# Sharing the weight sums of the wide products between GpSimd and VectorE

## The reference

```
proj = x @ w_in            # 1024 x 9240; among its parts: oa, zb, gate_a, gate_b
ha = mlstm(qa, ka, va, gates)                       # rms norm, then times sigmoid(oa)
hb = gated_delta(conv(qkv_b), beta, a)              # rms norm, then times silu(zb)
y  = sigmoid(gate_a) * (ha @ w_branch_a) + sigmoid(gate_b) * (hb @ w_branch_b)
x  = layernorm(alpha * x + y @ w_out)
x  = layernorm(alpha * x + (silu(gate) * up) @ w_ffn_down)   # gate, up = x @ w_ffn_up
```

## Time and profile before

| | us |
|---|---|
| median of 3 runs | 2968.23 (2964.52 to 2969.87) |
| the profiled execution | 2973.33 |
| its span | 2971.0 |
| TensorE busy | 2755.1 |
| VectorE busy | 1234.2 |
| ScalarE busy | 605.4 |
| GpSimd busy | 377.9 |

### The profile page before, as it was taken

One profiled execution on the slowest core, in us unless ns is written; L12 is line 12 of the kernel. 1 busy time (PEld: TensorE's weight loads), 2 busy tenths in 40 slices (PEclk: granted clock), 3 DMA queues, 4 the chain that ended last, 5 costly groups with the idle time before them and its releaser, 6 DMA issues.

```text
span 2971.0 us, 31547 instructions
## 1 busy us (share of the span) xinstructions
PE 2755.1 (93%) x12368; PEld 1548.1 (52%) x12368; DVE 1234.2 (42%) x2182; ACT 605.4 (20%) x1191; POOL 377.9 (13%) x359
## 2 busy tenths in 40 slices
PE   6998899999999998978787999999999999999998
PEld 3455564454434555534333586665445686664453
DVE  2546532222324554211111253553665444554675
ACT  1134311111111142111111113341110113430110
POOL 2100000000001000000000004654000006562000
PEclk8999889999999998988888899999999999999999
DMA  9324238999999345899999643134335433224342
GB/s 286 94 90 158 85 142 342 421 421 421 421 421 316 122 177 220 358 422 421 421 421 421 221 156 125 61 114 133 127 141 210 144 140 114 87 84 170 142 156 99
DMA packets 182658, 670.22 MB, mean 226 GB/s; under 512 B 8113, under 2 KB 18665, under 8 KB 133361
## 3 DMA queue, kind: packets, MB, share of 16 engines
q1 hardware_dynamic: 175696, 653.28, 56.8%
q0 software_dynamic: 6816, 14.94, 2.1%
HBM read 667.09 MB, written 2.90 MB: 226 GB/s over the span
## 4 chain that ended last, share of the span: by engine, by line
PE 70%; DMA 19%; DVE 6%; ACT 3%; issue 2%; POOL 0%; SPq 0%; DVEq 0%; ACTq 0%; POOLq 0%
DMA ring<-in_exp_w_up_dram 19%; PE bank L801 18%; PE bank L813 10%; PE bank L1507 9%; PE bank L1402 7%; PE bank L1567 4%; PE bank L1421 4%; PE bank L320 3%; PE bank L1022 3%; PE bank L1230 2%; PE bank L1074 1%; PE bank L961 1%; PE bank L843 1%; PE bank L983 1%; PE bank L769 1%
## 5 line engine op out<-in xcount | busy, mean ns | idle before, releaser
L813 PE MATMUL bank<-ring,arena 128*64 128x512 f32 (+1 forms) x2992 | 593.6, 637 | 94.4 <-DMA ring<-in_exp_w_up_dram 77.7
L813 PEld LDWEIGHTS bank<-ring,arena 128*64 128x64 f32 (+1 forms) x2992 | 174.2, 128 | 492.2 <-issue 408.6
L801 PE MATMUL bank<-ring,arena 128*128 128x512 f32 (+1 forms) x764 | 318.6, 577 | 1.6 <-ACT arena L457 1.5
L1507 PE MATMUL bank<-ring,arena 128*128 128x512 f32 (+1 forms) x672 | 267.1, 557 | 3.9 <-issue 3.3
L1402 PE MATMUL bank<-ring,arena 128*128 128x512 f32 x560 | 260.0, 597 | 1.3 <-ACT arena L2043 1.3
L801 PEld LDWEIGHTS bank<-ring,arena 128*128 128x128 f32 x764 | 144.7, 191 | 166.0 <-issue 163.9
L801 PE MATMUL bank<-arena,ring 128*128 128x256 f32 x1024 | 222.7, 379 | 0.0
L3164 POOL TENSOR_TENSOR ring<-ring 128x512 f32<-128x512 f32 x160 | 213.8, 1336 | 46.3 <-PE bank L1402 34.8
L801 PEld LDWEIGHTS bank<-arena,ring 128*128 128x128 f32 x1024 | 193.6, 189 | 28.9 <-issue 0.9
L1507 PEld LDWEIGHTS bank<-ring,arena 128*128 128x128 f32 x672 | 126.6, 190 | 137.7 <-issue 135.0
L2591 DVE COPY arena<-bank 128x512 f32<-128x512 f32 x64 | 44.3, 692 | 369.0 <-PE bank L813 368.2
(11 more groups left out here) (351 smaller groups left out, 2979.0 us busy)
## 6 DMA issues: line engine op xcount, KB each, us to landing
ring<-in_exp_w_down_dram SPq DMA_DIRECT2D x64, 2048.0 KB, 19.2
ring<-in_exp_w_up_dram SPq DMA_DIRECT2D x63, 2048.0 KB, 23.7
ring<-in_exp_w_gate_dram SPq DMA_DIRECT2D x60, 2048.0 KB, 22.6
ring<-in_w_in_dram SPq DMA_DIRECT2D x42, 2048.0 KB, 7.8
ring<-in_ada_w_dram SPq DMA_DIRECT2D x24, 2048.0 KB, 11.6
ring<-in_w_ffn_up_dram SPq DMA_DIRECT2D x20, 2048.0 KB, 8.0
ring<-in_w_ffn_down_dram SPq DMA_DIRECT2D x10, 2048.0 KB, 8.0
ring<-in_w_out_dram SPq DMA_DIRECT2D x8, 2048.0 KB, 10.1
```

Of the source, the lines that this page charges most:

```text
L801: last = mm(o, lhs(k), rhs(k), start=start and k == 0, stop=stop and k == kt - 1)
L813: last = mm(U(us[c])[g * rows:(g + 1) * rows, :], lhs(k), rhs(i, c), start=(k < parts), stop=(k >= KT - parts))
L1507: last = mm(U(u)[:, 0:n], lhs(k), rhs[:, k, 0:n], start=(k == 0), stop=(k == 3))
```

## The change

The two sums of the upper blocks stay on GpSimd. The two sums of the lower blocks leave GpSimd's program and become one VectorE instruction of 128x2048 each. They stand in VectorE's second fill step of p7, which had no work before. There VectorE waits for p3, for the two counts of `pool_sums` and for the arrival of both slots. They count on a new semaphore, `low_sums`, on which TensorE waits before p6 and p4; before p5 and p7 it waits on `pool_sums` as it did. GpSimd no longer waits for p3 before its additions, other than for its being copied out.

```diff
@@ TensorE, dense()
-                            if name in ("p5", "p7", "p6", "p4"):
+                            if name in ("p5", "p7"):
                                 nc.tensor.wait_ge(sem["pool_sums"], pe.due("pool_sums"))
+                            if name in ("p6", "p4"):
+                                nc.tensor.wait_ge(sem["low_sums"], pe.due("low_sums"))
@@ VectorE, dense()
                         first = FIRST_PART[i % 2]
+                        top0 = slot[arrived[l, (i, 0)][0]][:, 0:4, :]
+                        low0, low1 = (slot[arrived[l, (i, c)][0]][:, 4:8, :] for c in range(2))
                         for name in PRODUCTS:
                             yield
                             u = dv.unit(lane=DENSE)
                             if name == "p1":
                                 u_p1 = u
+                            elif name == "p3":
+                                u_p3 = u
+                            elif name == "p7":
+                                landed(u_p3)
+                                nc.vector.wait_ge(sem["pool_sums"], dv.due("pool_sums", 2))
+                                step(tt(low1, low1, top0, ALU.subtract), "low_sums")
+                                for c in range(2):
+                                    s, landed_at, _ = arrived[l, (i, c)]
+                                    nc.vector.wait_ge(sem[f"chunk{s}"], landed_at)
+                                step(tt(low0, low0, low1, ALU.subtract), "low_sums")
@@ GpSimd
                     by_rows(top[0], top[1], top[0])
                     by_rows(top[1], low[1], top[1])
-                    produced(us["p3"])
-                    by_rows(low[1], low[1], top[0])
-                    by_rows(low[0], low[0], low[1])
                     taken_out(us["p3"], us["p5"])
```

More of the change, by code:

```diff
@@ L218, in build @@
                   "w_sums", "x_sums", "gate_silu", "hid_ready", "hid_sums",
-                  "pool_step", "pool_sums", "pool_x", "pool_pre", "pool_out", "pool_gated", "dense_out"]
+                  "pool_step", "pool_sums", "low_sums", "pool_x", "pool_pre", "pool_out", "pool_gated", "dense_out"]
         sem = {n: ctx.enter_context(nc.semaphore(n)) for n in names}
```

## The result

The changed kernel takes 2977.41 us (2975.85 to 2986.46, 6 runs), the kernel before on the same chip 2967.89 (2958.68 to 2969.87, 6 runs). The ratio of the two is 1.0045, with a 95% interval of [1.0032, 1.0058]: slower by some 13 us (9.5 by the medians), and the interval doesn't hold 1. The forecast was 2987.

What follows compares the result with a forecast made beforehand. TensorE, busy 93%, was taken as the bound, so only its waits count. Per layer 0 + 0 + 1.65 - 0.8 + 6.9 + 1.8 = 9.55 us; two layers add 19.1 to 2968.2, giving 2987.3 us, range 2976 to 3004.

Steps and rivals of the forecast that it cites:

- the wait at W4 governs: Main forecast: at the fifth wide product TensorE waits for sums queued behind VectorE's gated heads; 2987 us, chance 0.79.
- W0 and W1: First and second wide products: VectorE's added sums fit without delaying TensorE; cost 0, bound 0 to 1 us each.
- W2: Third wide product: the sums and a slipped-in GpSimd addition delay a delta-rule step of TensorE by 1.65 us.
- W3, relief: Fourth wide product: without GpSimd's sums the delta rule's setup ends sooner; gain 2.0 to 3.05 us, taken as 2.5.
- W3, cost at the step: Fourth wide product: sums and a slipped-in addition delay TensorE's delta step by 1.7 us, 0.7 without the addition.
- W4, wait: Fifth wide product: p6 starts 6.9 us later, waiting for sums behind the gated heads; bounds 6.5 and 8.2.
- W4, slow clock behind it: Fifth wide product: after TensorE's 7.5 us idle, one slow-clock stretch costs 1.8 us; bounds 0 and 3.4.
- a net cost of 1: Fourth wide product: the unfavourable bound on relief and step cost together, against an expected net gain of 0.8 us.
- the fourth rival: First four wide products: the delta rule absorbs nothing, 2.7 us lost at each; 3007 us, chance 0.12.
- the fifth rival: Every wide product: VectorE's subtraction collides with or precedes GpSimd's first two sums; no chance of its own.
- The relief governing: Fourth wide product: delta-setup waits and the slow stretch go, saving 10 us; 2958 us, chance 0.03.
- The third rival: Whole stage: all is hidden or gains and costs cancel, the fifth product's stall being half; 2971 us, chance 0.06.

Runs made afterwards that it cites:

- e2: The changed kernel with the fifth wide product's two lower sums put back on GpSimd; 2963.82 us, ratio 0.9999 to the kernel before.
- e3: The kernel before with only the fifth wide product's two lower sums moved to VectorE; 2981.88 us, ratio 1.0053.
- e5: The changed kernel with the fifth wide product's two VectorE sums moved ahead of the gated heads, into an idle gap; 2966.71 us, ratio 1.0008 to the kernel before.
- e6: The changed kernel with GpSimd's addition behind p7 made to wait for both lower sums; 2981.0 us, ratio 1.0057 to the kernel before.
- e4: The kernel before with only the fourth wide product's two lower sums moved to VectorE; 2962.74 us, ratio 0.9996.
- e9: Kernel before with the fourth wide product's lower sums on VectorE, the second a step later, and the third's upper GpSimd sums delayed; 2954.39 us, ratio 0.9975.
- e1: The changed kernel measured again unchanged; 2984.47 us, ratio 1.0060 to the kernel before.
- e7: The kernel before with the fourth wide product's lower GpSimd sums held until the last delta block's setup is done; 2959.57 us, ratio 0.9995.
- e8: e7 with the third wide product's upper GpSimd sums also held until VectorE has gated the mLSTM's output; 2956.67 us, ratio 0.9983 to the kernel before.

## Why the prediction was right

**The forecast's case came: the wait at W4 governs.** The stages grew by 9.49 and 9.04 us, and the working had 9.55 per layer. The time alone would say less: 2977.4 lies near the low end of the range, 2976, and it is the stages and e2, e3 and e5 that show the mechanism. Term by term, forecast against measured in layer 0:

| term | forecast (bounds) | measured | shown by |
|---|---|---|---|
| W0 and W1 | 0 (0 to 2) | 0.20 | stage cuts |
| W2 | 1.65 (0.6 to 1.9) | 1.66 | e6: 0.73 without the slipped-in addition |
| W3, relief | -2.5 (-2.0 to -3.05) | -3.09 | e4: -1.68 with the clock fallen |
| W3, cost at the step | 1.7 (0.7 alone) | 1.78 | e4: 1.79; e6: 0.83 |
| W4, wait | 6.9 (6.5 to 8.2) | 6.85 | e3: 6.85; e2, e5: 0 in layer 0 |
| W4, slow clock behind it | 1.8 (0 to 3.4) | 2.09; layer 1: 1.59 | e3: 2.37 |

**W4.** The step that carried the forecast was to follow VectorE's program order and not its busy share of 42%: the sums stand behind the square, the root and the eight gated heads, and TensorE has nothing between the mixed steps and p6. The Trainium skill, "GPSIMD Engine Reference", section 4.1, sends such elementwise work to VectorE. The rows agree with it on the duration (one of 2292 ns for four of 1336) but the kernel got slower with it: 1.0045 with all five products moved; in e9, at 0.9975, one is moved, to a fitting place, and W2's sums on GpSimd are delayed. e2 and e5 show the place as the cause. Both remove some 8 to 9 us per layer, one by taking the sums off VectorE, the other by leaving them there in an earlier gap. e3 brings the loss without any other part. The slow clock behind the wait came out near the forecast partly by luck: I had one stretch of 3.41 us at 0.50, and 6.8 us came, of which only what lay behind the start of p6 cost anything (4.2 us in layer 0).

**W2.** The timelines of VectorE, GpSimd and TensorE behind W2's p7, against the earlier trace rows:

```profile
1925.58 2.29 DVE L2827 TENSOR_TENSOR ring<-ring 128x2048 f32<-128x2048 f32 x1
1927.91 3.24 DVE L2831 TENSOR_TENSOR ring<-ring 128x2048 f32<-128x2048 f32 x1
1931.18 0.42 DVE L2891 TENSOR_TENSOR ring<-ring,bank 128x256 f32<-128x256 f32 x1
...
1927.56 1.44 POOL L3178 TENSOR_TENSOR arena<-arena 128x512 f32<-128x512 f32 x1 [5.25 <-ACT arena L2045]
...
1931.66 0.71 PE L1476 MATMUL bank<-ring 128*128 128x128 f32 x4 [1.41 <-DVE ring L2891]
```

The addition is due at 1927.56, shortly before L2827 ends, and ends at 1929.0; the second sum starts by its record at 1927.91 and takes 3.24. Only then comes L2891, and TensorE's wait of 1.41 for it. This is the chain as the working had it.

**W3.** The timelines of VectorE and TensorE against the earlier trace rows:

```profile
1963.16 1.64 DVE L2872 TENSOR_TENSOR ring<-arena,ring 128x512 f32<-128x512 f32 x1
1967.00 0.69 DVE L2872 TENSOR_TENSOR ring<-arena,ring 128x512 f32<-128x512 f32 x1
1970.63 2.29 DVE L2827 TENSOR_TENSOR ring<-ring 128x2048 f32<-128x2048 f32 x1
1972.96 3.24 DVE L2831 TENSOR_TENSOR ring<-ring 128x2048 f32<-128x2048 f32 x1
1976.23 0.69 DVE L2884 TENSOR_TENSOR ring<-ring,bank 128x512 f32<-128x512 f32 x1
...
1976.98 1.16 PE L1423 MATMUL bank<-ring 128*128 128x128 f32 x8 [1.52 <-DVE ring L2884]
```

One L2872 still collides, with the one addition that GpSimd has left there; the other is down to 0.69. The relief came out at the upper end of its bounds since the clock held. I had taken the middle between held and fallen, which is right for what could be known: the trace of before shows only the fallen one, after an idle of 2.95. The 0.6 us per layer by which the relief came out above my 2.5 is thus the clock's doing; by 0.04 it is outside the bound of 3.05. It isn't shown to be chance: the clock held here in both layers of all five kernels that have the sums of W0 to W3 on VectorE (after, e1, e2, e5, e6), and fell in both layers of e4. What decides stays open. The bound on the other side, a net cost of 1, followed from neither term (2.0 and 1.7 leave a gain of 0.3); nothing came of it. So the slow stretch at W3 went away, and one came at W4.

**W0 and W1.** No gap opened at either; the fourth rival, which wanted 2.7 at each, is excluded. The 0.20 arises in W1 between p6 and p4, where two products of the mLSTM start some 0.1 us late each. The first of them, L1364, starts 0.06 us after VectorE ends L2779 (1884.29), which stands behind the two sums; in e6 that distance is again 0.06, L2779 is later still, since the held-back addition now hits L2776, and the 0.20 is 0.32. So W1 didn't fit quite as well as the working had it. The upper sums of W0 were over 7 us ahead of the step (1829.9 against 1836.92) and not the 10 that the fifth rival names for every product; it made no difference.

**The other rivals.** The relief governing (2958) would have needed VectorE some 6.8 us earlier at W4; its sums start at 2036.29, and the 2038.90 of the working is 2036.26 on the time scale of after (p7 of W4 starts at 2027.55 there, at 2030.19 before). The third rival had W4's stall at half of what was forecast, since the gated heads would go faster; they took 4.90 us for 4.91, and 6.85 refutes it. What e2 and e5 measure, 0.9999 and 1.0008, is what is left of the change without W4, and it is that rival's "gains and costs cancel": -3.09 against 0.20 + 1.66 + 1.78, so +0.6 per layer, as e2 and e5 have it in layer 0.

**Where the number was off.** The forecast was +19.1 us, the first measurement is +13.4 by its ratio (9.5 by the medians), the second +17.8. The sum of the stages is 18.5, within 0.6 of the forecast, so no term of the working was badly sized. The spans of the two profiled executions differ by 13.7 us, and the rest lies outside the stages: in the execution after, W0 of layer 0 starts 3.2 us earlier, and between the two stages it is another 1.7 us ahead. The second is a slow stretch of the execution before, which after doesn't have:

```profile
2308.00:2311.40 3.40, 1.15 (x8) 0.68 (x7) 3.24 (x5) 0.00 (x0) 0.00 (x0) 1.00 0.78 246
2311.40:2314.80 3.40, 3.01 (x7) 1.35 (x6) 2.85 (x6) 1.38 (x3) 0.00 (x0) 0.62 0.97 369
```

The change has no instruction at either place. The 3.2 us are scatter: W0 of layer 0 starts between 1799.4 and 1813.8 us in the eleven profiled executions, whose edits all lie behind that point. The 1.7 us are less clearly so. From the last matmul of W4 of layer 0 to W0 of layer 1 it takes 422.5 us in after, e1, e3 and e6, all four that have W4's wait, and in e9; in before, e2, e4, e5, e7 and e8 it takes 423.6 to 424.2. Whether the wait favours this place, or it is chance, stays open. Such places move the total of an execution by a few microseconds, as the runs of before do too (2958.68 to 2969.87).

## What to carry over

Price work that is moved to an in-order engine by the place in its queue: what stands ahead of it, and who waits for what stands behind. The same two instructions cost 9 us behind the gated heads (slow clock included), 1.7 to 1.8 behind a delta round, and nothing in a gap (e5) or split around the instruction that TensorE waits for (e9). Keeping GpSimd out of VectorE's way pays only where TensorE waits for the VectorE instruction that it hits, here two places in W2 and W3 worth 4.2 us per layer in e9; before work is moved in time, look at what it will run beside then (e7).

## What the runs showed of the hardware

**VectorE and GpSimd take turns by whole instructions when both inputs of the VectorE instruction lie in SBUF.** A 128x2048 subtraction takes 2292 ns alone and 3240 with one GpSimd addition in between; a 128x512 one 0.69 or 1.64 us; four 128x128 gated heads 1.52 or 4.31. One meeting with GpSimd adds up to 0.95 us to each of these, and 0.9 to 1.0 to three of the gated heads (0.35 alone); GpSimd's own instruction takes some 1.27 alone. The price goes by the instruction and not by its size. With one operand in PSUM nothing is added: L2855 takes 0.69 at 1967.12 in before, while GpSimd sums. The two 128x1024 products at L2785 go from 2176 to 1226 ns when GpSimd is held back (groups of e7, then of e8: total, mean ns, idle):

```profile
L2785 DVE TENSOR_TENSOR arena<-arena 128x1024 f32<-128x1024 f32 x2 | 4.4, 2176 | 0.1
```
```profile
L2785 DVE TENSOR_TENSOR arena<-arena 128x1024 f32<-128x1024 f32 x2 | 2.5, 1226 | 0.1
```

The Trainium skill, "SBUF — State Buffer", section "Who interferes with whom", calls the ports that the two engines share an exclusive lock, and says that a VectorE instruction with two SBUF inputs contends with a GpSimd instruction that reads SBUF. The rows above agree. What I had not expected is who loses most: a run of small instructions, which pays nearly once per instruction (four gated heads 2.8 us, as three of them were hit; one 128x2048 subtraction 0.95). I had not priced that for the gated heads in e7 and e8.

**The same idle time of TensorE doesn't always bring the slow clock.** At W3, 1.99 us of idle were followed by a slow stretch in both layers of e4 and in layer 1 of e7 (four matmuls in 3.58 and 2.97 us), and by full clock (1.88) in the change, in e9 and in layer 0 of e7. What decides isn't shown. A bound that has both cases is all that these runs allow there.

**A slow stretch costs by what of it lies behind the idle time.** The waits of 7.5 us at W4 were followed by the 1.2 GHz level in every run that has them (after, e1, e3), at a cost of 1.5 to 2.4 us; e6 waited 6.5 and paid 2.6. In layer 0 of the change the level lasts until 2042.80, 4.2 us behind the start of p6, and half of that, 2.1, is the cost.
